# Split sums of squares, split scores in every head, and a reordered mixing stage in one transformer layer

## The reference, cut to what matters

```python
x = x + 0.5 * swiglu(rms_norm(x, ffn1_norm), w1, w3, w2)          # FFN1, hidden 2816
h = rms_norm(x, mix_norm)
c_q, c_kv, k_pe, q_s, k_s, v_s = split(h @ w_in)                  # 384, 256, 32, 1024, 128, 128
y_mla = mla_attention(c_q, c_kv, k_pe, ...) @ w_o_mla             # 8 heads, 64 + 32 per head, block-causal
y_swa = swa_attention(q_s, k_s, v_s, rel_bias, sinks) @ w_o_swa   # 16 heads, band of two 64-token chunks
g_mla, g_swa = split(sigmoid(h @ w_gate))
x = x + (g_mla * y_mla + g_swa * y_swa) @ w_out
x = x + 0.5 * swiglu(rms_norm(x, ffn2_norm), ...)                 # FFN2
out = rms_norm(x, final_norm)

def rms_norm(x, g): return x * rsqrt(mean(x * x) + 1e-6) * g
```

## Time and profile before

| | us |
|---|---|
| median of three runs | 1111.98 |
| the three runs | 1111.95, 1111.98, 1112.8 |
| the profiled execution | 1112.14 |
| its span | 1110.4 |
| TensorE busy | 1103.0 (99%) |
| VectorE busy | 569.6 (51%) |
| ScalarE busy | 421.5 (38%) |
| GpSimd busy | 143.8 (13%) |

### The profile page before, as it was taken

The page is one execution under the profiler, slowest core; times in us unless marked ns, Lnnn a source line. Parts: engine busy times, 40 slices in busy tenths (PEclk is TensorE's granted clock), DMA queues, the critical chain, the costliest instruction groups (busy, mean ns, idle before and its releaser), DMA issues.

```text
span 1110.4 us, 14742 instructions
## 1 busy us (share of the span) xinstructions
PE 1103.0 (99%) x5184; PEld 900.1 (81%) x5184; DVE 569.6 (51%) x862; ACT 421.5 (38%) x730; POOL 143.8 (13%) x112
## 2 busy tenths in 40 slices
PE   9999999999999999999999999999999999999998
PEld 7888888888888887777778788888888888888896
DVE  6643344443445535865777654546443344434454
ACT  7322123322225424676756533444221223212243
POOL 0211011100113201321000002231110011100111
PEclk9999999999999999999999999999999999999999
DMA  7235322332224222152322222222233323322222
GB/s 266 85 99 122 107 95 94 95 95 94 96 78 129 95 97 74 32 121 86 102 70 77 76 95 95 95 95 95 94 95 99 104 100 94 95 95 95 85 86 76
DMA packets 35181, 107.73 MB, mean 97 GB/s; under 512 B 4272, under 2 KB 7504, under 8 KB 35136
## 3 DMA queue, kind: packets, MB, share of 16 engines
q1 hardware_dynamic: 34512, 105.82, 29.5%
q0 software_dynamic: 192, 0.78, 0.7%
q10 hardware_dynamic: 432, 0.54, 0.1%
HBM read 102.29 MB, written 2.88 MB: 95 GB/s over the span
## 4 chain that ended last, share of the span: by engine, by line
PE 98%; ACT 1%; DVE 0%; issue 0%; POOL 0%; DVEq 0%; POOLq 0%; ACTq 0%
PE bank L1484 29%; PE bank L1486 29%; PE bank L1485 29%; PE bank L1682 1%; PE bank L1706 1%; PE bank L1631 1%; PE bank L1692 1%; PE bank L1646 1%; PE bank L1850 1%; PE bank L1851 1%; PE bank L1852 1%; PE bank L1870 0%; PE bank L1868 0%; PE bank L1869 0%; PE bank L1654 0%; PE bank L1615 0%
## 5 line engine op out<-in xcount | busy, mean ns | idle before, releaser
L668 ACT ACTIVATE w_hi<-staged 128x1024 fp32r<-128x1024 f32 x182 | 193.1, 1061 | 542.3 <-PE bank L1486 542.1
L1484 PE MATMUL bank<-xg_hi,w_hi 128*128 128x512 f32 x1000 | 393.8, 394 | 0.3 <-ACT km L864 0.3
L1486 PE MATMUL bank<-xg_hi,w_lo 128*128 128x512 f32 x1000 | 389.5, 389 | 0.0
L1485 PE MATMUL bank<-xg_lo,w_hi 128*128 128x512 f32 x1000 | 389.4, 389 | 0.0
L1008 DVE TENSOR_TENSOR w_lo<-staged,w_hi 128x1024 fp32r<-128x1024 f32 x182 | 223.8, 1230 | 103.6 <-ACT w_hi L668 103.6
L1484 PEld LDWEIGHTS bank<-xg_hi,w_hi 128*128 128x128 f32 x1000 | 187.7, 188 | 44.5 <-issue 6.0
L1486 PEld LDWEIGHTS bank<-xg_hi,w_lo 128*128 128x128 f32 x1000 | 187.7, 188 | 39.4
L1485 PEld LDWEIGHTS bank<-xg_lo,w_hi 128*128 128x128 f32 x1000 | 187.8, 188 | 38.7 <-issue 0.7
L567 POOL TENSOR_TENSOR h_lo<-hid,h_hi 128x512 f32 x44 | 70.6, 1605 | 590.5 <-ACT h_hi L691 534.9
L1484 PE MATMUL bank<-h_hi,w_hi 128*128 128x512 f32 x304 | 118.4, 389 | 0.2 <-POOL h_lo L567 0.2
L1485 PE MATMUL bank<-h_lo,w_hi 128*128 128x512 f32 x304 | 118.3, 389 | 0.0
(11 more groups left out here) (222 smaller groups left out, 1038.8 us busy)
## 6 DMA issues: line engine op xcount, KB each, us to landing
staged<-in_ffn_w SPq DMA_DIRECT2D x118, 512.0 KB, 3.3
staged<-in_w_gate SPq DMA_DIRECT2D x16, 512.0 KB, 4.4
staged<-in_w_in SPq DMA_DIRECT2D x15, 512.0 KB, 3.3
staged<-in_ffn_w SPq DMA_DIRECT2D x16, 384.0 KB, 3.2
staged<-in_w_ob SPq DMA_DIRECT2D x8, 512.0 KB, 3.3
staged<-in_w_out SPq DMA_DIRECT2D x8, 512.0 KB, 3.3
x<-in_x_t SPq DMA_DIRECT2D x8, 256.0 KB, 4.6
staged<-in_w_oa SPq DMA_DIRECT2D x4, 512.0 KB, 3.3
```

The source lines that it names most:

```text
L668: nc.scalar.activation(w_hi[:, u % SPLIT, :], staged[:, u % STAGED, :], ACT.Copy).then_inc(hi_done, 1)
L1484: nc.tensor.matmul(o, wh, hi, start=start, stop=False)
L1485: nc.tensor.matmul(o, wh, lo, start=False, stop=False)
L1486: return nc.tensor.matmul(o, wl, hi, start=False, stop=stop)
```

## The change

1. NORM_X1 joins the split norms: its sum becomes two rounded products. The rounded ones are made by ScalarE in FFN1, and acc's upper half ahead of w_hi. VectorE makes the lower half behind unit 4's w_lo. For all three norms TensorE's first product now waits for the upper half alone.
2. The kv latent's sum and the turned rotary key become two rounded products each. Two new pieces, "squares" and "turned", make the halves in tile query_lo.
3. SPLIT_HEADS takes in heads 0 and 1. In every head ScalarE's rounding goes ahead of the exponential of the head's first tile, and VectorE's subtraction ahead of the next mask and maximum.
4. In the slots: uk's unit is split one slot earlier, uk's third group is read ahead of exponentials, q's sum goes behind uk's last group, and the gates' tanh with its table load moves from slots 16 and 17 to 14, 19 and 20. The split after one step of a pair is moved behind the next scores.
5. The first two band scores write the mask first and add the bias to the unmasked columns alone. normalise(4) moves into scores(5).
6. In the tail, Ln and Exp become one Abs_reciprocal_sqrt, its table loaded behind the first pass.

The diff, cut to its core:

```diff
-AHEAD_OF_EXP = (("uk", 1, 0),)
-
-
-
-EARLY_GATES = 5
+AHEAD_OF_EXP = (("uk", 1, 0), ("uk", 2, 0))
...
+EARLY_GATES, TANH_SLOTS = 5, (14, 14, 14, 19, 20)
...
-            [("kpe", 0, 0)] + halves("latent", 2),
+            [("kpe", 0, 0)] + halves("latent", 2) + [("squares", 0, "kv"), ("turned", 0, "kpe")],
...
-            [("rest", 0, "kv"), ("latent", 4, 1)],
+            [("rest", 0, "kv"), ("latent", 4, 1), ("split", 0, "uk")],
...
-            [("sum", 0, "q"), ("rest", 3, "q"), ("rest", 4, "q"), ("uk", 3, 0), ("gate", 2, 0)],
+            [("rest", 3, "q"), ("rest", 4, "q"), ("uk", 3, 0), ("sum", 0, "q"), ("gate", 2, 0)],
...
-            [("tanh", 0, "gate"), ("tanh", 1, "gate"), ("uv", 1, 0), ("uv", 2, 0)],
-            [("tanh", t, "gate") for t in range(2, EARLY_GATES)] + [("uv", 3, 0)]]
+            [("uv", 1, 0), ("uv", 2, 0)],
+            [("uv", 3, 0)]]
...
+    for t in reversed(range(EARLY_GATES)):
+        plan[TANH_SLOTS[t]].insert(0, ("tanh", t, "gate"))
...
-        SPLIT_NORMS = (NORM_MIX, NORM_X2)
+        SPLIT_NORMS = X_NORMS
...
+        PAIR_SPLIT = W_STEPS + 5
+        EARLY_SUMS = (1, 5)
...
-        SPLIT_HEADS = range(2, MH)
+        SPLIT_HEADS = range(MH)
...
             def x_norm_root(n, ahead=()):
                 nc.scalar.preload_act_table_set(LOG_EXP)
+                if n == NORM_X1:
+                    acc_hi(n)
                 for u in ahead:
...
-                        if of in SPLIT_NORMS:
+                        if of == NORM_X1:
+                            act.wait_ge(early_in, 16 * 2)
+                            nc.scalar.activation(one_rounded[:, :], one[:, :], ACT.Copy).then_inc(one_made, 1)
+                        else:
                             acc_hi(of)
...
+                elif kind == "squares":
+                    act.wait_ge(acc_done, sq_base[NORM_KV + 1])
+                    nc.scalar.activation(query_lo[:, 0, :], acc[:, NORM_KV % 2, :], ACT.Copy).then_inc(kv_hi_done, 1)
+                elif kind == "turned":
+                    act.wait_ge(const_in, 16 * 5)
+                    nc.scalar.activation(query_lo[:, 4, 0:P], turn_sb[:, :], ACT.Copy)
+                    act.wait_ge(grp_read, g + GROUP_AT["kpe", 0] + 1)
+                    nc.scalar.activation(query_lo[:, 2, :], rot[:, :], ACT.Copy).then_inc(rot_hi_done, 1)
...
+                for h in SPLIT_HEADS:
+                    if n + 2 == first_step(h):
+                        head_hi(h)
                 if (n % 2 == 0 or n + 2 >= W_STEPS) and n + 2 < STEPS:
                     exponentials(n + 2)
...
+                        nc.scalar.preload_act_table_set("abs_reciprocal_sqrt_and_small")
                 act.wait_ge(row_var, j + 1)
-                nc.scalar.activation(tok_log[:, j:j + 1], tok_var[:, j:j + 1], ACT.Ln).then_inc(row_log, 1)
-                act.wait_ge(row_log, j + 1)
-                nc.scalar.activation(tok_root[:, j:j + 1], tok_log[:, j:j + 1], ACT.Exp, scale=-0.5).then_inc(row_root, 1)
+                nc.scalar.activation(tok_root[:, j:j + 1], tok_var[:, j:j + 1], ACT.Abs_reciprocal_sqrt)\
+                    .then_inc(row_root, 1)
...
-                        if n in SPLIT_NORMS:
+                        if u:
                             acc_lo(n)
-                        if u:
                             split_lo(u + SPLIT)
                             split_lo(u + 1 + SPLIT)
                         else:
                             split_lo(2 * SPLIT)
+                            acc_lo(n)
                         make_rms(n)
...
-                    done(nc.vector.tensor_tensor(tiles, tiles, bias[:, :, kv, :], ALU.add))
+                    first = CHUNK if c == 0 else 0
                     if c == 0:
-                        done(nc.vector.memset(tiles[:, :, 0:CHUNK], NEG))
+                        nc.vector.memset(tiles[:, :, 0:CHUNK], NEG)
+                    done(nc.vector.tensor_tensor(tiles[:, :, first:], tiles[:, :, first:], bias[:, :, kv, first:], ALU.add))
                     done(nc.vector.tensor_reduce(smax[:, n % 2, :], tiles, AX.X, ALU.max, negate=True))
-                    if n == 1:
-                        normalise(0)
+                    if n in EARLY_SUMS:
+                        normalise(n - 1)
...
+                if n + 1 < STEPS and n + 2 not in EARLY_SUMS:
...
-                    scores(n + 2)
                     for h in SPLIT_HEADS:
                         if n + 1 == first_step(h):
                             head_lo(h)
-                    split_next(PLAN[n])
+                    scores(n + 2)
+                    if n == PAIR_SPLIT + 1:
+                        split_next(PLAN[n - 1])
+                    if n != PAIR_SPLIT:
+                        split_next(PLAN[n])
...
             def sum_x_squares(n):
-                if n in SPLIT_NORMS:
-                    pe.wait_ge(one_made, 1)
-                    pe.wait_ge(acc_lo_done, SPLIT_NORMS.index(n) + 1)
-                    nc.tensor.matmul(bank[RMS_BANK][:, :], one_rounded[:, :], acc_split[:, 0, :], start=True, stop=False)
-                    nc.tensor.matmul(bank[RMS_BANK][:, :], one_rounded[:, :], acc_split[:, 1, :], start=False, stop=True)\
-                        .then_inc(ss_ready, 1)
-                    return
-                pe.wait_ge(early_in, 16 * 2)
-                sum_all(n, bank[RMS_BANK], ss_ready)
+                pe.wait_ge(one_made, 1)
+                pe.wait_ge(acc_hi_done, SPLIT_NORMS.index(n) + 1)
+                nc.tensor.matmul(bank[RMS_BANK][:, :], one_rounded[:, :], acc_split[:, 0, :], start=True, stop=False)
+                pe.wait_ge(acc_lo_done, SPLIT_NORMS.index(n) + 1)
+                nc.tensor.matmul(bank[RMS_BANK][:, :], one_rounded[:, :], acc_split[:, 1, :], start=False, stop=True)\
+                    .then_inc(ss_ready, 1)
...
-                if i == 0 or h not in SPLIT_HEADS:
+                if i == 0:
...
+                    pe.wait_ge(rot_lo_done, 1)
+                    for of in range(2):
+                        last = nc.tensor.matmul(o[:, :], query_lo[:, 4, 0:P], query_lo[:, 2 + of, :], start=of == 0,
+                                                stop=of == 1)
+                    last.then_inc(grp_ready, 1)
...
+                elif kind == "sum" and part == "kv":
+                    o = next_bank(gg)[:, :]
+                    pe.wait_ge(kv_lo_done, 1)
+                    nc.tensor.matmul(o, one_rounded[:, :], query_lo[:, 0, :], start=True, stop=False)
+                    nc.tensor.matmul(o, one_rounded[:, :], query_lo[:, 1, :], start=False, stop=True)\
+                        .then_inc(grp_ready, 1)
```

More of the change, by code:

```diff
@@ L226, in trunk_layer @@
             acc_end = sb("acc_end", [P, HALF], f32, ffn)
[L227 removed]
+            tok_sq, tok_part, tok_var, tok_root, tok_half, tok_rstd = (
                 sb(n, [P, 2 * ROW_TILES], f32, ffn) for n in
[L229 removed]
+                ("tok_sq", "tok_part", "tok_var", "tok_root", "tok_half", "tok_rstd"))
         mix = ctx
@@ L290, in trunk_layer @@
         one_made, acc_hi_done, acc_lo_done = sem("one_made"), sem("acc_hi_done"), sem("acc_lo_done")
+        kv_hi_done, kv_lo_done = sem("kv_hi_done"), sem("kv_lo_done")
+        rot_hi_done, rot_lo_done = sem("rot_hi_done"), sem("rot_lo_done")
         lat_log, lat_rooted, lat_step, lat_scaled = sem("lat_log"), sem("lat_rooted"), sem("lat_step"), sem("lat_scaled")
@@ L889, in split_next @@
                         split_hi(u + used_up(*piece) + SPLIT)
-            act.wait_ge(early_in, 16 * 2)
-            nc.scalar.activation(one_rounded[:, :], one[:, :], ACT.Copy).then_inc(one_made, 1)
             acc_hi(NORM_MIX)
@@ L924, in _ @@
                         filler(*piece)
-                for h in SPLIT_HEADS:
-                    if n + 2 == first_step(h):
-                        head_hi(h)
             split_next(PLAN[STEPS])
@@ L1273, in filler @@
                     split_lo(u + UNIT_AT[part, t])
+                elif kind == "squares":
+                    dve.wait_ge(kv_hi_done, 1)
+                    nc.vector.tensor_tensor(query_lo[:, 1, :], acc[:, NORM_KV % 2, :], query_lo[:, 0, :].bitcast(f32),
+                                            ALU.subtract).then_inc(kv_lo_done, 1)
+                elif kind == "turned":
+                    dve.wait_ge(rot_hi_done, 1)
+                    nc.vector.tensor_tensor(query_lo[:, 3, :], rot[:, :], query_lo[:, 2, :].bitcast(f32),
+                                            ALU.subtract).then_inc(rot_lo_done, 1)
                 elif kind == "newton":
@@ L1526, in from_hidden @@
                 return h_hi[:, k, :], h_lo[:, k, :]
-            def sum_all(n, b, signal):
-                pe.wait_ge(acc_done, sq_base[n + 1])
-                nc.tensor.matmul(b[:, :], ones_32 if n != NORM_X1 else one[:, :], acc[:, n % 2, :],
-                                 start=True, stop=True).then_inc(signal, 1)
             def sum_x_squares(n):
-                if n in SPLIT_NORMS:
```

(19 more changed lines are left out.)

3 lines of the change are left out of this document (1 added, 2 removed).

## The result

| | us |
|---|---|
| before, median of 12 runs beside it | 1112.02 |
| changed, median of 12 runs | 1114.09 (1113.68 to 1115.57) |
| ratio | 1.0018, 95% interval 1.0011 to 1.0026 |
| forecast | 1112.0, range 1110.4 to 1114.1 |

The changed kernel is slower by 2.07 us, 0.19%. The interval lies above 1, but the difference is within the 0.2% that the prediction set as its bound for "slower" (1114.2). The time lies in the range by 0.01 us. It is close to the time that rival (a) gave, 1114.3, and not to the forecast's.

What follows compares the result with a forecast made beforehand. TensorE, busy 1103.0 of 1110.4 us, was taken to bound the kernel. Terms +2.65 -0.70 -0.74 +0.10 -0.27 -0.49 -0.36 -0.20 summed to -0.01, giving a median of 1112.0, range 1110.4 to 1114.1.

Steps and rivals of the forecast that it cites:

- rival (a): First norm's sum: TensorE's wait of about 3.0 us brings its clock to the lower level; 1114.3 us, chance 0.15.
- The wait: First norm's sum: the second rounded product waits for VectorE's subtraction behind unit 4's w_lo, shifting later products by +2.65 us.
- step 5: First band scores: the bias add covers half the columns, so TensorE waits less; -0.36 us.
- (2): Kv sum and turned key: rounded products replace float32 ones, -0.35 us each, -0.70 together.
- (4): Moved splits and evictions: uk's first product -0.27 us, the gate's product -0.49 us.
- (3): Heads 0 and 1: rounded score tiles save 0.74 us; a wait for head 1's subtractions adds 0.1 us.
- (6): Tail: one function replaces Ln and Exp, with its table load behind the first pass; -0.2 us.
- Step 7: Tanh table load and three tanhs fit ScalarE's 3.61 us idle stretch ahead of 518.47; cost 0.
- case (d): ScalarE's moved tanh group: the table load costs more than its row shows; 1112.8 us, chance 0.04.
- (c): Heads: new roundings and subtractions pile up and TensorE waits in places; 1113.0 to 1114.3 us, chance 0.08.
- a shift of 4 or more at 40: Sign in the changed profile: TensorE's products 4 us or more later at 40 us would mean rival (a).
- if that cover were gone: Kv sum: its halves arrive 0.9 us before needed; without that cover the kv sum would wait.

Runs made afterwards that it cites:

- experiment 6: Changed kernel with the first norm's subtraction ahead of unit 4's w_lo, and heads 0 and 1 with float32 scores again: 1110.01 us.
- experiment 4: Kernel before with only the first norm's sum split, its subtraction behind unit 4's w_lo: 1116.54 us, ratio 1.0035.
- experiment 3: Changed kernel with 4 further products ahead of the first norm's sum, to shorten TensorE's idle time: median 1114.03 us.
- experiment 2: Changed kernel with 13 further products ahead of the first norm's sum, keeping TensorE at work through the wait: 1112.54 us.
- experiment 7: Changed kernel with the first norm's subtraction ahead of w_lo, and kv sum and turned key as float32 products again: 1109.95 us.
- experiment 10: Changed kernel with the first norm's subtraction ahead of w_lo, and each head's lower halves ahead of normalising its first tile: 1109.35 us.

## Why the prediction was right and where it failed

Right: what bounds the kernel, and that part 1 costs more than it saves. The wait was put at TensorE's second sum product, for the subtraction, starting near 26.0; it started at 25.68, with the first product of the sum 0.31 sooner than before. The parts that save came out near their sizes: -0.35 for -0.36 (step 5), -0.75 for -0.70 (2), -0.96 for -0.76 (4), -0.56 for -0.74 (3), -0.21 for -0.2 (6). Step 7 held too, in ScalarE's rows of the changed kernel:

```profile
517.31 1.28 ACT L902 ACT_TABLE_LOAD   x1
518.61 1.67 ACT L902 ACTIVATE gates<-gates 128x512 f32<-128x512 f32 x3
520.92 0.60 ACT L825 ACTIVATE probs_t<-bank 128x512 f32<-128x512 f32 x1 [0.64 <-PE bank L1713]
```

The first tanh follows the load by 1.30, and 0.64 of idle time is left. No drain beside the load shows, so case (d) did not happen; no run shows the 0.8 us that it added.

That the measured time lies in the range is luck. The range's upper end, 1114.1, was put there for cases (c) and (d), and (a), the case that came true, was left out of it. By the sign that the prediction gave for (a), a shift of 4 or more at 40, it is (a): the shift there is 4.1.

Failed: the choice between the forecast and rival (a). The step was the inference from the earlier trace rows. TensorE stopped at 1104.85 and its clock fell at about 1109.6, and I took 4.8 us as a bound below which a pause is safe, and gave (a) 0.15. It is one draw of a delay that varies. The kernel's end alone shows that. Worked out as for the earlier trace rows, the fourteen profiled executions put the fall 2.0 to 5.3 us after the last product's end. The shortest is experiment 6's, with the clock down at about 1104.8:

```profile
1102.34 0.39 PE L1899 MATMUL bank<-end_hi,h_lo 128*128 128x512 f32 x1
```

```profile
1104.00:1105.00 1.00, 0.00 (x0) 0.00 (x0) 0.93 (x4) 0.62 (x1) 0.00 (x0) 0.88 0.00 0
```

In experiment 4 the clock was down at 25.0, some 2.1 us after the sum's first product ended, and in experiment 3 a pause of 2 us lost it in 7 of 11 runs by their times and mean clocks. The price in (a), 2.4 less what overlaps, was about half too high for the changed kernel (1.55 by experiment 2), and below the 2.8 of the profiled execution of experiment 4. The Trainium skill, in "TensorE: Matmul & The Clock Gate", section "What's actually happening", had said that the gate watches recent activity in windows that run free of the kernel. I read from that rule that it is a matter of phase whether a pause is caught. The traces fit it: one pause of 2.90 us, clock down from 26.05 to 29.46 in one execution and from 25.0 to 31.8 in another. The phase itself no run here shows.

Failed by a smaller sum: step 2's "if that cover were gone". I looked only at the kv sum's own readers, where the halves do arrive in time, and not at what stands behind them in VectorE's queue. The two subtractions make VectorE 0.7 late, it has next to no idle time until that point, and a w_lo that was just in time before is not: +0.48, shown by experiment 7. Step 3's wait was +0.28 and not +0.10; experiments 6 and 10 show that it is that wait.

The bookkeeping, from the forecast's -0.01: the wait +0.29 (2.94 for 2.65), the clock +1.43, w_lo +0.48, the head's wait +0.18, the savings together -0.07, the start -0.31. That makes +2.0, which is the difference of the two profiled executions (1114.12 - 1112.14); the medians give +2.07.

## What to carry to other kernels

Where one engine is at 99%, price a new wait of that engine twice: its length, and what the clock does behind it. A pause of 2.9 us cost 1.55 us more than its length here, which is more than any one of the savings that came with it. When two steps on a feeder engine are independent, put first the one whose reader stands ahead in the bounding engine's queue: swapping two lines was worth 4.6 us. A delay that is read once, as that of the clock's fall at the kernel's end, is one draw and no bound. And follow an addition on a feeder to its next idle stretch, not only to its own reader.

## What the hardware did that I had not expected

TensorE's granted clock fell at about 26.05 in the changed kernel, 0.4 us behind a pause of 2.9 us, and 2.1 us into the same pause in experiment 4's execution. At the kernel's end it held for 4.8 us after the last product before the change, and for 2.0 to 5.3 us over all fourteen profiled executions. Once low, it stayed at half for 3.4 us in the changed kernel, with TensorE at work throughout, and for 6.8 us in experiment 4, with TensorE at work for all but the first 0.8. Rounded products of 512 columns have a pitch of 0.43 us at that level and 0.23 at the upper one.
